# Reporting a code page of TensorE by a sequencer increment ahead of its first product, instead of by the second product of the page

## The reference, cut to what matters

```
def swiglu(x, w_gate, w_up, w_down):
    return (jax.nn.silu(x @ w_gate) * (x @ w_up)) @ w_down

def moe_swiglu(h, router_w, w_gate, w_up, w_down):
    logits = (xt @ router_w).astype(jnp.float32)
    top_val, top_idx = lax.top_k(logits, TOP_K)          # 2 of 8 experts
    gates = jax.nn.softmax(top_val, axis=-1)
    ...
    for e in range(N_EXPERTS):
        y = y + combine[:, e:e + 1] * swiglu(xt, w_gate[e], w_up[e], w_down[e])
```

## Time and profile before

| | before |
|---|---|
| median of 3 runs | 1592.11 us (1589.5 to 1596.15) |
| span of the profiled execution | 1591.7 us |
| PE busy | 1517.8 us, 95% of the span |
| PEld busy | 1330.8 us, 84% |
| DVE, ACT, POOL busy | 16%, 11%, 9% |
| HBM traffic | 270 GB/s over the span, 360 to 390 GB/s in the expert stage |

### The profile page before, as it was taken

The page is one execution under the profiler, slowest core; times in us unless marked ns, Lnnn a source line. Parts: engine busy times, 40 slices in busy tenths (PEclk is TensorE's granted clock), DMA queues, the critical chain, the costliest instruction groups (busy, mean ns, idle before and its releaser), DMA issues.

```text
span 1591.7 us, 54543 instructions
## 1 busy us (share of the span) xinstructions
PE 1517.8 (95%) x25973; PEld 1330.8 (84%) x25973; DVE 256.7 (16%) x489; ACT 179.0 (11%) x383; POOL 143.6 (9%) x167
## 2 busy tenths in 40 slices
PE   8999999999999999999999999999999999999997
PEld 7787587777687865989999999899999999998996
DVE  3433310000143435000010010010000000000102
ACT  3233120000131322100000000000000000000001
POOL 2243200000022532200000000000000000000000
PEclk9999999999999999999999999999999999999999
DMA  9213244444242245999999999999999999999992
GB/s 335 89 53 133 106 159 159 159 159 146 92 161 106 76 154 229 360 377 376 363 374 376 357 348 376 356 382 369 365 376 366 370 367 369 367 355 373 389 379 88
DMA packets 133612, 433.48 MB, mean 272 GB/s; under 512 B 9082, under 2 KB 33916, under 8 KB 119052
## 3 DMA queue, kind: packets, MB, share of 16 engines
q1 hardware_dynamic: 132384, 427.70, 71.9%
q0 software_dynamic: 672, 2.14, 0.4%
q10 hardware_dynamic: 332, 0.13, 0.0%
HBM read 428.89 MB, written 1.05 MB: 270 GB/s over the span
## 4 chain that ended last, share of the span: by engine, by line
PE 92%; issue 3%; DVE 2%; ACT 1%; POOL 1%; DMA 0%; ACTq 0%; DVEq 0%
PE ps L1133 35%; PE ps L1157 18%; PE ps L982 9%; PE ps L681 8%; PE ps L993 4%; PE ps L844 4%; PE ps L692 3%; PE ps L1190 2%; PE ps L1062 1%; PE ps L801 1%; PE ps L714 1%; PE ps L677 1%; PE ps L811 1%; PE ps L707 1%; PE ps L821 1%
## 5 line engine op out<-in xcount | busy, mean ns | idle before, releaser
L1157 PE MATMUL ps<-LT_sb,ring 128*64 128x88 f32 x5376 | 218.4, 239 | 16.2 <-issue 15.1
L1157 PEld LDWEIGHTS ps<-LT_sb,ring 128*64 128x64 f32 x5376 | 212.0, 137 | 21.7 <-issue 19.4
L1133 PE MATMUL ps<-wpost,ring 128*64 128x88 f32 x5376 | 217.0, 240 | 12.4 <-issue 10.9
L1133 PE MATMUL ps<-AT_sb,ring 128*64 128x88 f32 x5376 | 217.0, 239 | 9.9 <-issue 9.7
L1133 PEld LDWEIGHTS ps<-wpost,ring 128*64 128x64 f32 x5376 | 210.9, 138 | 17.5 <-issue 15.4
L1133 PEld LDWEIGHTS ps<-AT_sb,ring 128*64 128x64 f32 x5376 | 211.7, 138 | 14.6 <-issue 13.9
L982 PEld LDWEIGHTS ps<-hT_sb,ring 128*128 128x128 f32 x768 | 136.0, 190 | 24.6 <-issue 9.1
L982 PE MATMUL ps<-hT_sb,ring 128*128 128x256 f32 (+1 forms) x768 | 155.7, 362 | 0.0
L681 PE MATMUL ps<-hT_sb,ring 128*128 128x256 f32 x576 | 128.2, 380 | 0.0
L681 PEld LDWEIGHTS ps<-hT_sb,ring 128*128 128x128 f32 x576 | 108.1, 190 | 15.0 <-issue 0.5
L1985 POOL TENSOR_SCALAR small<-small 128x1 f32<-128x1 f32 x16 | 3.9, 241 | 1203.3 <-ACT late L1513 933.6
(11 more groups left out here) (284 smaller groups left out, 1156.5 us busy)
## 6 DMA issues: line engine op xcount, KB each, us to landing
ring<-in_moe_w_gate SPq DMA_DIRECT2D x84, 1024.0 KB, 8.4
ring<-in_moe_w_up SPq DMA_DIRECT2D x84, 1024.0 KB, 8.0
ring<-in_moe_w_down SPq DMA_DIRECT2D x84, 1024.0 KB, 8.2
late<-in_moe_w_up SPq DMA_DIRECT2D x28, 1024.0 KB, 8.5
late<-in_moe_w_gate SPq DMA_DIRECT2D x28, 1024.0 KB, 7.7
late<-in_moe_w_down SPq DMA_DIRECT2D x28, 1024.0 KB, 8.0
ring<-in_ffn_w_gate SPq DMA_DIRECT2D x11, 1024.0 KB, 5.4
ring<-in_ffn_w_up SPq DMA_DIRECT2D x11, 1024.0 KB, 8.1
```

The source lines that it names most:

```text
L1133: ins = mm(o[lo:lo + P // 2, :], pairs[:, m % 2, lo:lo + P // 2], xgT[e % 2][:, k, :], start=(k == 0 and m % 4 == 0), stop=(k == KD - 1), ...
L1157: ins = mm(o[lo:lo + P // 2, :], d[:, i, m * P + lo:m * P + lo + P // 2], moe_hid[:, 2 * j + i, :], start=(first and m % 4 == 0), stop=las ...
```

## The change

Each page is reported by an instruction of its own on PE, `pe.sem_inc(page_turn, 1)`, placed before the call that would be the first whole one of the page. No product carries the report any more. Everything else of the kernel stays. `page_turns` counts the new instruction too (`at += 1`).

```
-TURN_MARKS = (8,)
+TURN_MARK = 0
...
 def page_turns():
-    def place(n):
-        return n // len(TURN_MARKS) * PAGE + TURN_MARKS[n % len(TURN_MARKS)]
-
     at, turns, free_at, used_at = FIRST_IN_PAGE - WAITS["g0"], set(), [], []
-    passed = sum(m < FIRST_IN_PAGE for m in TURN_MARKS)
...
             for i in range(first, first + calls):
+                if at >= (1 + len(turns)) * PAGE + TURN_MARK:
+                    turns.add((owner, name, i))
+                    at += 1
                 at += size
...
-                if at >= place(passed + len(turns)) and not has_signal:
-                    turns.add((owner, name, i))
...
-            def turned(ins, e, block, call):
+            def turn(e, block, call):
                 if (e, block, call) in PAGE_TURNS:
-                    ins.then_inc(page_turn, 1)
+                    pe.sem_inc(page_turn, 1)
...
                             for lo in (0, P // 2):
+                                turn(e, f"{kind}{c}", call)
                                 ins = mm(o[lo:lo + P // 2, :], pairs[:, m % 2, lo:lo + P // 2],
                                          xgT[e % 2][:, k, :], start=(k == 0 and m % 4 == 0), stop=(k == KD - 1),
                                          skip_group_check=True)
-                                turned(ins, e, f"{kind}{c}", call)
                                 call += 1
```

More of the change, by code:

```diff
@@ L1092, in gather @@
                         for n in range(3):
+                            turn(e, "gather", call)
                             ins = gather_part(j, k, t, n, t == 0 and n == 0, t == 1 and n == 2)
-                            turned(ins, e, "gather", call)
                             call += 1
@@ L1102, in onehot_transposes @@
                 for t in range(TT):
+                    turn(e, "oh", t)
                     ins = mm(bank(6)[0:SLOTS, t * P:(t + 1) * P], onehot[e % 2][:, t, :], ident_bf, start=True, stop=True)
-                    turned(ins, e, "oh", t)
                 ins.then_inc(ohT_ps, 1)
@@ L1156, in m_down @@
                             for lo in (0, P // 2):
+                                turn(e, f"d{c}", call)
                                 ins = mm(o[lo:lo + P // 2, :], d[:, i, m * P + lo:m * P + lo + P // 2],
@@ L1159, in m_down @@
                                          skip_group_check=True)
-                                turned(ins, e, f"d{c}", call)
                                 call += 1
@@ L1170, in y_transposes @@
                 for m in range(KD):
+                    turn(e, "y", m)
                     ins = nc.tensor.transpose(bank(6 + m // 4)[0:SLOTS, m % 4 * P:(m % 4 + 1) * P], yT[:, m, :], ident)
-                    turned(ins, e, "y", m)
                 ins.then_inc(yT_ps, 1)
@@ L1189, in scatter_piece @@
                 for n, lo in enumerate((0, P // 2)):
+                    turn(e, "s", 2 * i + n)
                     ins = mm(bank(6 + hf)[lo:lo + P // 2, quarter * 256:(quarter + 1) * 256],
@@ L1193, in scatter_piece @@
                              start=(quarter == 0), stop=True, skip_group_check=True)
-                    turned(ins, e, "s", 2 * i + n)
                 if quarter:
```

## The result

The changed kernel is slower: 1629.88 us median of 6 runs (1626.12 to 1638.85) against 1594.1 us, the median of 6 runs of the kernel before, ratio 1.024, 95% interval 1.022 to 1.027. The forecast was 0.8% faster.

The account below looks back on a forecast made before the run. DMA engines bound the expert stage. 1591.7 - 14 (idle time) + 1 (more single-load pages) - 1.6 (shorter tail) + 0 (instructions) + 2 (read order) = 1579.1, with 0.4 for the median 1579.5 us; range 1570 to 1612.

Parts of the forecast that it names:

- What bounds the kernel: Expert stage: DMA engines bound it, busy 0.97 at 369 GB/s; PE's stalls are how it waits for them.
- The page read waits behind the loads issued before it: At page starts: piled-up loads delay the next code page's read, 4.1 us in the page at 960.48.
- The report moves forward: At page starts: an increment reports about 0.4 us earlier after a stall, 1.1 us earlier without one.
- The size of the gain: In 18 pages that follow a single-load page: 14 us of DMA idle time removed, bounds 3 and 19.
- the idle time moves: Rival for the 18 pages: a later report sets the next page, earlier loads wait longer, time near 1590; chance 0.2.
- 174 more instructions: On PE's sequencer: increments of 51 ns each are covered by its lead or by waits; 0 us, bounds 0 and 5.
- The order of read and loads: At page starts: a page's first load now and then gets ahead of the page read; 2 us of loss.
- the first load overtakes: Slower rival at page starts: first load precedes the page read in nearly every page, 70 us more; chance 0.2.

Follow-up runs that it names:

- e1: Changed kernel with TURN_MARK 6 instead of 0, all increments 3 to 10 instructions behind the real page edge; 1590.06 us, 0.9996 of the kernel before.
- e5: Changed kernel with TURN_MARK 3 instead of 0, increments 0 to 7 instructions behind the real page edge; 1589.51 us, 0.998 of the kernel before.
- e10: The kernel of e5 (TURN_MARK 3) measured again; 1588.88 us, 0.9996 of the kernel before.
- e4: Kernel before, products still reporting, plus 174 increments of an unused semaphore where the changed kernel has its reports; 1594.15 us, ratio 1.002.
- e2: Changed kernel with TURN_MARK -6 instead of 0, all increments 3 to 11 instructions ahead of the real page edge; 1715.17 us, 1.079 of the kernel before.
- e9: Increment 3 to 11 instructions ahead of the edge releases a page's first load, product behind it the second; 1670.49 us, 1.050 of the kernel before.

## Why the prediction was wrong

- *What bounds the kernel*: right. The DMA engines do. The 40 us of the changed kernel's span are 42 us of their idle time, and in every variant PE's stalls went with it.
- *The page read waits behind the loads issued before it*: right, and it is what the loss is made of.
- *The report moves forward*, "an increment there" when "the sequencer reaches the new page": this step failed. It took the planner's page for the real one. The reports of before stand 3 to 15 instructions inside the page and so did not show the difference, but its stalls stand at the real edge: counted against the program they would have. 88 of 174 increments stood in the old page. From there the report does not come 0.4 or 1.1 us earlier but, if the next page is late, earlier than the whole stall (2.4 us before the page in the example). Its loads are then in line before the read that follows the page's start, and not behind it. e1 against the changed kernel shows it: 6 instructions back, 2.5%.
- *The size of the gain*, 14 us of idle time in 18 pages: far too large, even with every report inside its page. In e5 SP's first load came 0.7 us earlier in pages after a one-load page that began without a stall (1.1 taken) and 0.45 us in those that began with one (0.4 taken). The idle time fell less than that, from 1.08 to 0.62 us a page without a stall and from 1.09 to 0.95 with one. In sum it fell in these pages from 20.0 to 15.5 us (e1), 15.6 (e5) and 18.3 (e10) in the profiled executions, and in the other pages it rose from 1.5 to about 7 to 11. By the medians of e1, e5 and e10 nothing is left. This is the outcome of the second rival, "the idle time moves"; why the other pages lost what these gained was not isolated, so its reason is not shown.
- *174 more instructions*: 0 taken, 5 as the bound, about 3 measured (e4).
- *The order of read and loads*: 2 us taken. The race inside the page did not show: as close as 0 to 7 instructions behind the edge, 0.02 loads were ahead (e5). The rival "the first load overtakes" had its cause wrong, as e1 shows, but named what happens once a report stands in the old page. Its price was too low: 70 us for all pages and "0 to 20 us" for half of them; measured 123 (e2) and 36 us. It took the middle, 5.8 us a page, and e2's pages took 6.07. It said the harm decides only once more than half of the pages are overtaken. It starts earlier, because a stall puts the report still earlier against its page (1.20 loads ahead after a stall, 0.20 without), so that 42 of 44 such pages stalled the next.
- *Arbitration between queues.* The Trainium skill ("DMA: Bandwidth & Descriptors", Queues, rings and completion order) has each DMA engine go round robin between its queue rows at packet boundaries. By that rule e1, e2 and e9 would be alike. e2 and e9 are 8 and 5% slower than e1, and the read on q8 starts when the loads of q1 in front of it have been started. The measurement decides: between these two queues an earlier load had an earlier place in line.
- *Page crossings.* The Trainium skill ("Runtime: NRT & Kernel Launch", Instruction fetch mechanics) calls the cost of crossing a page mostly hidden. The trace does not agree: e2 stalls at some 146 of 174 crossings, 171 us in all.

## What to carry to other kernels

Where PE's program is read page by page while the DMA engines are full, as here, a load was cheap just behind the page edge and dear just ahead of it. Put such a mark some instructions behind the edge, as a margin for the count, and verify it against where the stalls stand, not against the planner. An earlier signal is not better when what it releases queues in front of something its sender needs. And a rival with a threshold should be priced with the feedback in it: when a stall makes the next stall more likely, half of the pages cost more than they seem to.

## What the runs showed of the hardware

- The read of the next code page takes its place in line when PE enters a page: in pages after a stall 1.48 loads are ahead of it when the report stands 3 to 11 instructions before the edge, 0.02 when it stands 0 to 7 behind (e2, e5).
- A sequencer increment on PE takes 51 ns. It runs ahead of the array: in e5 SP's first load goes out 0.2 to 0.3 us before the page's first weight load where PE did not stall. It does not run ahead across a page that is not there: after a stall the load goes out 0.1 us behind that weight load.
- With few loads in front, a page read began 1.1 us (982.87 before) and 1.3 us (1008.71 after) after the page's start, and PE had no gap at the next edge.
- After a page read ends, a PE that has stalled goes on 1.4 us later in the mean (1.2 to 1.6), in the kernel before and in e2.
